# Expert weights in transfers of 64 partitions by 8 KB instead of 128 partitions by 4 KB

## The chip, the core and the metric

The kernel runs on one NeuronCore of a Trainium2 chip. The metric is the device time of one execution in microseconds (us). "The profile" is one profiled execution of the same program; its rows are counted in us from its first instruction. Engines: PE is TensorE (matmuls; PEld its weight loads), DVE is VectorE, ACT is ScalarE, POOL is GpSimd, SP is SyncE, which here does nothing but issue transfers. Transfers run on the core's 16 DMA engines.

## What is computed

Two blocks over 256 tokens of width 1024, float32 throughout. The first block has two layers, each a sequence mixer (a gated recurrence, then stick-breaking attention) with memory attention beside it, an output projection with a norm, and a mixture of experts with a norm. The second block is one layer of attention with forget gates, a convolutional feed-forward of width 2816 and a gated embedding. The change touches the weights of the mixture of experts alone:

```python
def hier_moe(x, w_group, b_group, w_router, b_router, w_gate, w_up, w_down):
    # top-1 of 4 groups, then top-2 of its 4 experts: gates (T, 16)
    ...
    h = jax.nn.silu(jnp.einsum('td,edf->tef', xf, w_gate)) * jnp.einsum('td,edf->tef', xf, w_up)
    y = jnp.einsum('tef,efd->td', h * gates[:, :, None].astype(h.dtype), w_down)
```

w_gate and w_up are 16 x 1024 x 256 and w_down is 16 x 256 x 1024, for each of the two layers: 3 MB an expert, 48 MB a layer, all of it fetched from device memory once.

## The kernel before, in words

**Engines and order.** Each engine runs one instruction stream written out by hand, in the order of the layers, and the streams meet at semaphores. SP's stream is the order of all weight transfers. `put` (from line 384) fetches the dense weights into a ring of four 1 MB buffers, `raw` (128 partitions by four slots of 2048 floats); ACT rounds each into `w_hi` (line 1639) and DVE takes the rest into `w_lo` (line 2116), and PE multiplies with both parts.

**The expert stage.** The expert weights are used unsplit, so `raw`, `w_hi` and `w_lo` together serve as twelve 1 MB *slabs* (`hi_as_raw` and `lo_as_raw` are the latter two seen as plain float32). `STREAM` (lines 72 to 77) lists the 48 slabs of a layer: for each of the 8 pairs of experts two halves of the gate and up weights of both experts ("G", four slabs), then the down weights of both experts of the pair before ("D", two slabs). SP's `experts` (line 392) walks through it. For slab n it waits until the buffer is free: for the first twelve until the dense weights there are used up (`lo_split`, `half_used`), and beyond until PE has used slab n - 12 and its neighbour (`slab_used`). Slabs 10 and 11 of layer 0 wait for `counted` besides. Then it issues two transfers of 512 KB that both count on the slab's semaphore, 16 each:

```python
if kind == "G":
    for i in range(2):
        cs = slice(HALF // 2 * i, HALF // 2 * i + HALF // 2)
        sp.dma_start(r[:, cs], gate_up[e, half, :, cs]).then_inc(landed, 16)
else:
    v = r.rearrange("p (k n) -> p k n", k=2)
    for i in range(2):
        sp.dma_start(v[:, i, :], wd[e, :, i, :]).then_inc(landed, 16)
```

Each covers all 128 partitions and half of every partition's row, so one run of bytes is 4 KB. `gate_up` has been laid out by the host as it lands (16 experts x 2 halves x 128 partitions x 2048); `w_down` is read as it is given, where partition p of slab half k is row 128 k + p.

**PE in the stage.** `short_path` runs `gate_up(p)` and then `down(p - 1)` for the eight pairs. Both wait (`weights_in`) until both slabs of a pair of experts have landed in full, 32 counts a slab. A slab takes 4 matmul steps for either expert, the two experts side by side in the two halves of the array; between them PE gathers the tokens of the next pair and scatters the results of the last (`hooks`). After `down(7)`, `close_sums` adds the last pairs up from `y_hi` and `y_lo`, which ACT (line 1639) and DVE (line 2137) make from PE's sums.

**After the stage.** SP goes on with `put`: in layer 0 with `w_kv_shared`, in layer 1 with `attn_w_in_2` (after the 256 KB of `p_2`). In ACT's stream the rounding of the first of these weights stands ahead of the last `y_hi`. The two rows of norm gains (`gain<-in_ln_ffn_g` and `_b`, 512 KB each) come on ACT's own queue while the first slabs are fetched.

Of the kernel before, what the change touches and what calls it, by code (L numbers as in the profile page):

```python
# [27 lines left out]
P = 128  # L28
# [24 lines left out]
HALF = 2048  # L53
# [55 lines left out]
def both(n):  # L109

    return n - n % 2 + 2
# [101 lines left out]
def build(nc, a, out, FAST_LIMIT=SLOTS):  # L213
    ctx = ExitStack()
    with ctx:
# [12 lines left out]
        def sem(name):  # L228
            if name not in sems:
                sems[name] = ctx.enter_context(nc.semaphore(name))  # L230
            return sems[name]
# [108 lines left out]
        def slab(layer, n):  # L340

            part, slot = kept_at(layer, n % SLABS)
            return {"raw": raw, "hi": hi_as_raw, "lo": lo_as_raw}[part][:, slot, :]

        def slab_sem(layer, n):

            part, slot = kept_at(layer, n % SLABS)
            return raw_in[slot] if part == "raw" else slab_in[n % SLABS - RING]
# [8 lines left out]
        def _(sp):  # L357
# [35 lines left out]
            def experts(layer):  # L393

                base = AT[f"E{layer}"]
                assert h == base
                gate_up = a["gate_up"][layer]
                wd = a["w_down"][layer].rearrange("e (k p) n -> e p k n", p=P)
                for n, (kind, e, half) in enumerate(STREAM):
                    s = n % SLABS  # L400
                    if layer == 0 and n == SLABS - 2:
                        sp.wait_ge(sem("counted"), 2)
                    if n >= SLABS:
                        sp.wait_ge(slab_used, len(STREAM) * layer + both(n - SLABS))
                    elif s < RING:
                        sp.wait_ge(lo_split, base - RING + s + 1)
                    else:
                        sp.wait_ge(half_used, base - RING + (s - RING) // 2 + 1)
                    r, landed = slab(layer, n), slab_sem(layer, n)
                    if kind == "G":  # L410
                        for i in range(2):
                            cs = slice(HALF // 2 * i, HALF // 2 * i + HALF // 2)
                            sp.dma_start(r[:, cs], gate_up[e, half, :, cs]).then_inc(landed, 16)
                    else:
                        v = r.rearrange("p (k n) -> p k n", k=2)
                        for i in range(2):
                            sp.dma_start(v[:, i, :], wd[e, :, i, :]).then_inc(landed, 16)

            def gains(g, b, n):

# [8 lines left out]
            for c in range(2):  # L429
                cs = slice(512 * c, 512 * c + 512)  # L430
# [17 lines left out]
            for layer in range(2):  # L448
                if layer:
                    for half in range(2):  # L450
                        put(tm(a["w_kv_shared"], SEQ_W, half))
                    put(fm(a["w_kv_shared"], SEQ_W + 512))
                    for j in range(3):
                        put(fm(a["w_kv_shared"], 256 * j))
                        put(fm(a["b_w_in"][0], 256 * j))
                        if j == 0:
                            put(fm(a["b_w_in"][0], SEQ_W))
                    for half in range(2):
                        for j in range(2):
                            put(tm_rows(a["w_o"][1], 512 * j, O_ROWS[1][half]))  # L460
                else:
                    for half in range(2):
                        for j in range(2):
                            put(tm(a["w_o"][0], 512 * j, half))
                    put(fm(a["w_mem_kv"][1], 0))
                    sp.wait_ge(sem("mixed_ready"), 4)
                gains(a["ln_mix_g"][layer], a["ln_mix_b"][layer], 2 * layer)
                experts(layer)
# [28 lines left out]
            for n, (b, at, width) in enumerate(GATE_TILES):  # L497
                sp.wait_ge(sem("result"), n + 1)
                cs = slice(at, at + width)
# [1610 lines left out]
        def _(dve):  # L2110
# [773 lines left out]


_FULL = ["x", "mem", "a_w_in", "a_gnorm", "b_w_in", "w_kv_shared", "w_mem_kv", "w_o", "ln_mix_g", "ln_mix_b",
         "ln_ffn_g", "ln_ffn_b", "w_down", "p_2", "attn_w_in_2", "attn_b_f_2", "attn_w_out_2",
         "ln_mix_g_2", "ln_mix_b_2", "ffn_w_up_2", "ffn_w_down_2", "ln_ffn_g_2", "ln_ffn_b_2", "ple_w_proj_2",
         "ple_w_gate_2", "ple_b_gate_2"]

# [36 lines left out]
```

## Time and profile before

| | |
|---|---|
| time, median of 3 runs | 907.32 us (905.35 to 909.91) |
| span of the profiled execution | 902.7 us; its time was not taken apart from it |
| PE busy | 881.5 us (98%) |
| PE weight loads | 678.2 us (75%) |
| DVE, ACT, POOL busy | 502.8, 391.4, 35.2 us |
| TensorE clock granted | 1.00 of full speed |
| read from device memory | 203.87 MB, 227 GB/s over the span |
| queue of SP | 202.14 MB, 62.6% of the time of 16 DMA engines |

The span runs from the first to the last instruction. What a run takes around it (start and end of the program) is not in the trace: the three runs lie 2.7 to 7.2 us above this span, the median 4.6 us. The page cuts the span into 40 slices of 22.6 us and gives for each the busy share of each engine in tenths, the granted TensorE clock and what the DMA engines moved. A PE that is busy has something in its pipeline; a chain of waits names what the end of the program hung on.

### The profile page before, as it was taken

Reading aid. Unit: us, or ns where it says so; the run is one execution under the profiler, and the core shown is the slowest. Engines: PE = TensorE matmul, PEld = TensorE weight load, DVE = VectorE, ACT = ScalarE, POOL = GpSimd, SP = SyncE. Lnnn points to the kernel's source line nnn. Section 1 sums busy time; section 2 is a strip of 40 time slices with the busy share of each in tenths; the row PEclk is TensorE's granted clock in tenths of the full one; section 3 lists DMA queues with packets and bytes.
Section 4 is the critical chain, followed back from the end, with each engine's and each line's share of the span. In section 5 each row is a group of like instructions: output and inputs, shape, how many; then the busy total and the mean of one; then the engine's idle time right before and its main releaser. Section 6 shows DMA issues by size and latency. Waiting matters only on the chain.

```text
span 902.7 us, 13442 instructions
## 1 busy us (share of the span) xinstructions
PE 881.5 (98%) x5387; PEld 678.2 (75%) x5387; DVE 502.8 (56%) x752; ACT 391.4 (43%) x531; POOL 35.2 (4%) x73
## 2 busy tenths in 40 slices
PE   7999999989999999999999999999999999999998
PEld 6988998944543698878545446899877888888887
DVE  4798876711111965626211118465658777777576
ACT  4755654232221536551322215435545666655441
POOL 7100010000000000000000000000001000000010
PEclk9999999999999999999999999999999999999999
DMA  9934417979999574329599996354543655546611
GB/s 319 318 96 139 141 47 263 341 254 411 409 409 401 179 242 169 100 89 351 190 411 409 409 403 216 122 181 166 176 152 118 219 192 192 187 139 233 234 47 46
DMA packets 102828, 205.78 MB, mean 228 GB/s; under 512 B 6896, under 2 KB 57840, under 8 KB 102768
## 3 DMA queue, kind: packets, MB, share of 16 engines
q1 hardware_dynamic: 101184, 202.14, 62.6%
q10 hardware_dynamic: 1584, 2.81, 1.0%
q8 instruction: 42, 0.69, 0.3%
q14 instruction: 18, 0.15, 0.0%
HBM read 203.87 MB, written 1.05 MB: 227 GB/s over the span
## 4 chain that ended last, share of the span: by engine, by line
PE 83%; DVE 5%; DMA 5%; ACT 4%; issue 2%; SPq 1%; DVEq 0%; ACTq 0%
PE psum L709 80%; DVE w_lo L2116 2%; DMA raw<-in_w_kv_shared 2%; ACT w_hi L1639 1%; DMA raw<-in_attn_w_in 1%; DMA raw<-in_a_w_in 1%; ACT arena L1639 1%; SPq L361 1%; PE psum L817 1%; DMA x_res<-in_x 1%; ACT x_slots L1639 0%; PE psum L1504 0%; PE psum L922 0%; DVE xt L2137 0%; PE psum L1018 0%
## 5 line engine op out<-in xcount | busy, mean ns | idle before, releaser
L709 PE MATMUL psum<-xt,w_hi 128*128 128x256 f32 (+1 forms) x1056 | 253.8, 321 | 3.9 <-DVEq L2831 1.7
L2116 DVE TENSOR_TENSOR w_lo<-raw,w_hi 128x2048 fp32r<-128x2048 f32 x88 | 200.7, 2287 | 47.4 <-ACT w_hi L1639 44.3
L709 PE MATMUL psum<-xt,w_lo 128*128 128x256 f32 x704 | 198.2, 282 | 0.0
L709 PEld LDWEIGHTS psum<-xt,w_hi 128*128 128x128 f32 x1056 | 177.1, 190 | 19.4 <-issue 2.7
L1639 ACT ACTIVATE w_hi<-raw 128x2048 fp32r<-128x2048 f32 (+1 forms) x90 | 170.1, 1892 | 38.8 <-PE psum L709 23.4
L709 PEld LDWEIGHTS psum<-xt,w_lo 128*128 128x128 f32 x704 | 134.1, 191 | 0.0
L709 PE MATMUL psum<-w_hi,xt 128*128 128x512 f32 (+1 forms) x368 | 112.8, 379 | 0.0
L1639 ACT ACTIVATE arena<-psum 128x512 f32<-128x512 f32 (+2 forms) x70 | 40.8, 601 | 124.9 <-PE psum L709 82.6
L709 PE MATMUL psum<-hi_as_raw,x_slots 128*64 128x512 f32 x176 | 80.8, 596 | 0.0
L709 PE MATMUL psum<-lo_as_raw,x_slots 128*64 128x512 f32 x176 | 80.8, 596 | 0.0
L709 PEld LDWEIGHTS psum<-w_hi,xt 128*128 128x128 f32 x368 | 67.3, 189 | 12.6 <-DVE xt L2137 1.1
L2601 DVE SCALAR_TENSOR_TENSOR arena<-psum,slot_gate,arena 128x256 f32<-128x256 f32 x16 | 7.7, 484 | 114.8 <-ACT arena L1639 114.8
L709 PE MATMUL psum<-w_hi,mt_hi 128*128 128x512 f32 (+1 forms) x184 | 69.8, 380 | 0.3 <-DVE mt_lo L2137 0.3
L709 PE MATMUL psum<-w_lo,xt 128*128 128x512 f32 (+1 forms) x184 | 68.4, 372 | 0.0
L709 PE MATMUL psum<-w_lo,mt_hi 128*128 128x512 f32 (+1 forms) x184 | 68.3, 371 | 0.0
L709 PE MATMUL psum<-w_hi,mt_lo 128*128 128x512 f32 (+1 forms) x184 | 68.3, 371 | 0.0
L1639 ACT ACTIVATE arena<-arena 128x512 f32<-128x512 f32 (+3 forms) x62 | 40.3, 656 | 57.2 <-DVE arena L2245 22.7
L709 PEld LDWEIGHTS psum<-hi_as_raw,x_slots 128*64 128x64 f32 x176 | 23.0, 137 | 44.4 <-issue 43.3
L582 POOL TENSOR_TENSOR rstd<-var_eps,neg_half 128x1 f32<-128x1 f32 (+1 forms) x15 | 16.5, 1104 | 838.6 <-DVE var_eps L2389 586.5
L709 PE MATMUL psum<-arena 128*128 128x128 f32 (+2 forms) x316 | 40.5, 302 | 2.9 <-DVE arena L2265 1.0
L2137 DVE TENSOR_TENSOR y_lo<-psum,y_hi 128x512 fp32r<-128x512 f32 x32 | 21.7, 689 | 36.5 <-ACT y_hi L1639 36.5
L709 PEld LDWEIGHTS psum<-arena 128*128 128x128 f32 (+1 forms) x316 | 34.3, 189 | 8.9 <-issue 3.4
(267 smaller groups left out, 1245.0 us busy)
## 6 DMA issues: line engine op xcount, KB each, us to landing
hi_as_raw<-in_gate_up SPq DMA_DIRECT2D x44, 512.0 KB, 7.7
lo_as_raw<-in_gate_up SPq DMA_DIRECT2D x44, 512.0 KB, 9.1
raw<-in_ffn_w_up SPq DMA_DIRECT2D x44, 512.0 KB, 4.5
raw<-in_gate_up SPq DMA_DIRECT2D x40, 512.0 KB, 6.8
raw<-in_a_w_in SPq DMA_DIRECT2D x26, 512.0 KB, 7.5
raw<-in_w_down SPq DMA_DIRECT2D x24, 512.0 KB, 10.5
raw<-in_attn_w_in SPq DMA_DIRECT2D x24, 512.0 KB, 5.0
raw<-in_ffn_w_down SPq DMA_DIRECT2D x22, 512.0 KB, 4.1
```

The costliest lines, as they stand in the source:

```text
L361: sp.dma_start(dst, src).then_inc(raw_in[slot], 16)
L582: pool.tensor_tensor(rstd[:, cols], var_eps[:, cols], neg_half[:, cols], ALU.pow)\
L709: return pe.matmul(o, l, r, start=start, stop=stop, skip_group_check=skip)
L817: last = pe.transpose(turned(b)[:, k // 4, k % 4, :], x_res[:, b, P * k:P * k + P], ident[:])
L1639: return act.activation(o, i, f, **kw)
L2116: return dve.tensor_tensor(w_half(h, w_lo), w_half(h, raw), w_half(h, w_hi).bitcast(F32), ALU.subtract).then_inc(lo_split, 1)
L2137: return dve.tensor_tensor(o, whole, hi.bitcast(F32), ALU.subtract)
L2601: dve.scalar_tensor_tensor(ex_h[:, p % 2, 0, :], psum[:, gu_bank(p), 256:512], slot_gate[:, p // 2 % 2, p % 2:p % 2 + 1], ex_s[:, p % 2, 0 ...
```

## The change

The columns are no longer halved, the partitions are: each slab now comes as one transfer into partitions 0 to 63 and one into partitions 64 to 127, each with the whole row of 2048 floats (8 KB) of every partition. For this the host lays out the down weights like the others, as `down` (2 x 16 x 128 x 2048). Number, size and order of the transfers, their semaphores and all waits stay.

```diff
@@ -395,7 +395,7 @@
                 base = AT[f"E{layer}"]
                 assert h == base
                 gate_up = a["gate_up"][layer]
-                wd = a["w_down"][layer].rearrange("e (k p) n -> e p k n", p=P)
+                down = a["down"][layer]
                 for n, (kind, e, half) in enumerate(STREAM):
...
                     r, landed = slab(layer, n), slab_sem(layer, n)
-                    if kind == "G":
-                        for i in range(2):
-                            cs = slice(HALF // 2 * i, HALF // 2 * i + HALF // 2)
-                            sp.dma_start(r[:, cs], gate_up[e, half, :, cs]).then_inc(landed, 16)
-                    else:
-                        v = r.rearrange("p (k n) -> p k n", k=2)
-                        for i in range(2):
-                            sp.dma_start(v[:, i, :], wd[e, :, i, :]).then_inc(landed, 16)
+                    src = gate_up[e, half] if kind == "G" else down[e]
+                    for i in range(2):
+                        ps = slice(P // 2 * i, P // 2 * i + P // 2)
+                        sp.dma_start(r[ps, :], src[ps, :]).then_inc(landed, 16)
@@ -2905,6 +2901,8 @@
+    down = np.asarray(inputs["w_down"]).reshape(2, 16, 2, 128, 1024).transpose(0, 1, 3, 2, 4)
+    arrays["down"] = np.ascontiguousarray(down).reshape(2, 16, 128, 2048)
```

SP's stream at the head of layer 0's expert stage, before: a row is a number of like transfers in a row, with the partitions and floats of one (`gain` is the norm gains just ahead of the stage, the two rows left out repeat those above them, `in_w_down` and `in_gate_up` are the weights in device memory).

```order
L424 DMA gain<-in_ln_mix_b 128x1024
L413 DMA raw<-in_gate_up 128x1024 x8
L413 DMA hi_as_raw<-in_gate_up 128x1024 x2
L413 DMA lo_as_raw<-in_gate_up 128x1024 x2
...
L417 DMA hi_as_raw<-in_w_down 128x1024 x2
L417 DMA lo_as_raw<-in_w_down 128x1024 x2
```

The same place in the changed kernel:

```order
L420 DMA gain<-in_ln_mix_b 128x1024
L413 DMA raw<-in_gate_up 64x2048 x8
L413 DMA hi_as_raw<-in_gate_up 64x2048 x2
L413 DMA lo_as_raw<-in_gate_up 64x2048 x2
...
L413 DMA hi_as_raw<-in_down 64x2048 x2
L413 DMA lo_as_raw<-in_down 64x2048 x2
```

Every transfer of the stage stands in its old place with its new shape; nothing moves past anything, and the streams of the other four engines read alike before and after.

## Rows read from the trace of the kernel before

**Rows 1.** The page: busy time, and the span in 40 slices.
```profile
PE 881.5 (98%) x5387; PEld 678.2 (75%) x5387; DVE 502.8 (56%) x752; ACT 391.4 (43%) x531; POOL 35.2 (4%) x73
...
GB/s 319 318 96 139 141 47 263 341 254 411 409 409 401 179 242 169 100 89 351 190 411 409 409 403 216 122 181 166 176 152 118 219 192 192 187 139 233 234 47 46
```

**Rows 2.** Stretches: us, then busy us of each engine, clock, DMA share, GB/s.
```profile
20.00:30.00 10.00, 10.00 (x86) 10.00 (x86) 5.65 (x6) 4.79 (x4) 4.59 (x8) 1.00 1.08 360
180.00:190.00 10.00, 6.90 (x59) 5.00 (x59) 2.15 (x9) 5.95 (x10) 0.00 (x0) 1.00 0.37 125
200.00:289.00 89.00, 89.00 (x485) 41.72 (x482) 14.55 (x28) 17.37 (x34) 0.00 (x0) 1.00 1.03 409
455.00:540.00 85.00, 85.00 (x466) 40.46 (x464) 14.55 (x28) 16.54 (x32) 0.00 (x0) 1.00 1.03 408
```

**Rows 3.** The chain of waits, layer 0's expert stage: start us, us, what.
```profile
227.71 15.07 PE psum L709 x89
242.78 0.22 PE psum L1196 x2
243.00 14.64 PE psum L709 x74
257.64 0.22 PE psum L1196 x2
...
277.71 0.38 SPq L361
278.09 0.04 issue
278.13 13.92 DMA raw<-in_w_kv_shared
292.05 0.02 issue
292.07 1.07 ACT w_hi L1639
```

**Rows 4.** Waits of SP's queue from 195 to 290: total, times, longest.
```profile
SPq L413 <- PE psum L709: 35.8, 10, 6.7
SPq L417 <- PE psum L709: 12.2, 6, 3.9
```

**Rows 5.** The last four w_down transfers of layer 0 (274 to 277).
```profile
L417 SPq DMA_DIRECT2D lo_as_raw<-in_w_down x2: 430/896/1362, 275.1 to 275.5; - x2
...
DMA to landing us min/median/max: 9.7/11.8/13.8
```

**Rows 6.** The last eight w_down transfers of layer 1 (519 to 530).
```profile
L417 SPq DMA_DIRECT2D lo_as_raw<-in_w_down x4: 430/432/432, 520.0 to 527.0; - x4
...
DMA to landing us min/median/max: 8.9/11.2/13.4
```

**Rows 7.** Timeline of PE: down(7) begins, and what follows it (both layers).
```profile
289.46 0.59 PE L709 MATMUL psum<-hi_as_raw,ht 128*64 128x512 f32 x1
...
294.52 0.50 PE L709 MATMUL psum<-y_hi,ht_lo 128*128 128x512 f32 x1 [1.08 <-ACT y_hi L1639]
295.24 0.50 PE L709 MATMUL psum<-y_lo,ht_lo 128*128 128x512 f32 x1 [0.22 <-DVE y_lo L2137]
...
540.95 0.59 PE L709 MATMUL psum<-hi_as_raw,ht 128*64 128x512 f32 x1
...
545.71 0.50 PE L709 MATMUL psum<-y_lo,ht_lo 128*128 128x512 f32 x1 [0.23 <-DVE y_lo L2137]
```

**Rows 8.** Timeline of ACT at the end of layer 0's stage.
```profile
292.07 1.91 ACT L1639 ACTIVATE w_hi<-raw 128x2048 fp32r<-128x2048 f32 x1 [2.01 <-DMA raw<-in_w_kv_shared]
293.89 1.07 ACT L1639 ACTIVATE y_hi<-psum 128x512 fp32r<-128x512 f32 x2
```

**Rows 9.** Timeline of SP, the starts of both streams: start us, us for all.
```profile
144.44 9.21 SPq L413 DMA_DIRECT2D raw<-in_gate_up  x8
...
185.39 0.80 SPq L413 DMA_DIRECT2D hi_as_raw<-in_gate_up  x2
...
190.91 2.45 SPq L413 DMA_DIRECT2D raw<-in_gate_up  x4
...
406.54 0.80 SPq L413 DMA_DIRECT2D hi_as_raw<-in_gate_up  x2
...
442.40 1.95 SPq L413 DMA_DIRECT2D raw<-in_gate_up  x4
```

**Rows 10.** The raw, hi and lo gate_up transfers from 144 to 168.
```profile
DMA to landing us min/median/max: 4.1/6.5/9.4
```

More of the change, by code:

```diff
@@ L2886 @@
 _FULL = ["x", "mem", "a_w_in", "a_gnorm", "b_w_in", "w_kv_shared", "w_mem_kv", "w_o", "ln_mix_g", "ln_mix_b",
-         "ln_ffn_g", "ln_ffn_b", "w_down", "p_2", "attn_w_in_2", "attn_b_f_2", "attn_w_out_2",
+         "ln_ffn_g", "ln_ffn_b", "p_2", "attn_w_in_2", "attn_b_f_2", "attn_w_out_2",
          "ln_mix_g_2", "ln_mix_b_2", "ffn_w_up_2", "ffn_w_down_2", "ln_ffn_g_2", "ln_ffn_b_2", "ple_w_proj_2",
```

## The prediction

> **What bounds the kernel now.** First the page: PE is busy in 98% of the span, and the bandwidth line has two plateaus of 401 to 411 GB/s, four slices each, which are the expert stages of the two layers [rows 1]. Everywhere else it lies lower. Then the stretches: in both plateaus PE is busy for the whole stretch while the DMA engines are busy for the whole stretch too, a share of 1.03 at 409 and 408 GB/s [rows 2]. So two engines are full at once, and the question is which has slack. PE takes 14.64 + 0.22 us for one pair of experts and 15.07 + 0.22 for another, about 15.1 on average [rows 3]. A pair is six slabs, twelve transfers of 524,288 bytes; at 409 GB/s one takes 1.28 us and twelve take 15.4. The supply is thus slower than the demand, and only the ring of twelve slabs, filled before the stage begins, carries the stage to its end. SP still waits for PE to free slabs, 35.8 + 12.2 us between 195 and 290 [rows 4], but no longer for want of work for the DMA engines: their queue stays full. How much of the lead is left at the end: the last down weights of layer 0 are issued at 275.5 and land 13.8 us later, at 289.3 [rows 5], and down(7), which needs them, begins at 289.46 [rows 7]. In layer 1: 527.0 at the latest and 13.4, so 540.4 [rows 6], against 540.95 [rows 7]. **The transfers have 0.1 and 0.5 us of slack.** Whatever makes a transfer longer is paid in full, and whatever makes it shorter can only give back the waits behind it. Those are small: the next weights land at 292.05 at the end of the chain's transfer of 13.92 us [rows 3], ACT rounds them first for 1.91 us and makes y_hi after that [rows 8], and PE waits 1.08 + 0.22 us for y_hi and y_lo in layer 0 and 0.23 in layer 1 [rows 7].
>
> **What changes.** 96 transfers a layer keep their bytes, order and waits. Two properties change: a run of bytes is 8 KB and not 4, and a transfer touches 64 partitions and not 128. Everything else is priced at nothing: the host's layout of the down weights is done before the launch, the other engines' streams are the same, and issuing is SP's work, 0.80 us for two [rows 9], beside transfers that take longer.
>
> *The longer run.* A stretch of 1 KB runs (a_w_in, behind a full queue) moves 360 GB/s and one of 4 KB runs 409 [rows 2]. Sixteen engines side by side: 1024 x 16 / 360 = 45.5 ns a run and 4096 x 16 / 409 = 160.2 ns. The line through both is 7.3 ns a run and 0.0373 ns a byte, which gives 313 ns for 8 KB, 418 GB/s, 1.253 us a transfer: 2% less. Slabs 10 to 47 of a layer follow each other without a gap (they start at 185.39 in layer 0 [rows 9]), 76 transfers, so the end would come 76 x 0.027 = 2.1 us earlier. Of it PE sees only its waits behind the stage, 1.3 + 0.2 = 1.5 us.
>
> *Half the partitions.* No row of this trace has a transfer of 64 partitions. What the rows say is that nearly all rates tend to one ceiling, which the line above puts at 16 / 0.0373 = 429 GB/s for endless runs. A ceiling per byte sits either in the DMA engines themselves, and then it doesn't matter where they write, or on the way into the partitions, and then a transfer that writes to half of them has half of it. The bounds: 1.25 us a transfer (only the run counts) and twice today's 1.28, 2.56 us. The trace can't choose. The Trainium skill (SBUF — State Buffer, "Door 1: The DMA port swizzle") holds that the second is so: partitions 0 to 63 lie behind 8 of 16 ports, and it gives 196 GB/s for them against 328 for all 128. By that figure a transfer would take 2.67 us, and the sum below would be 223 us and the time 1130. Its section "Can I just issue two DMAs to hit both halves?" adds that two such transfers side by side gained 6%, as they serialize. No run here shows either yet.
>
> I take the ceiling to be on the way in, since the change alternates between the halves and nothing in the kernel makes engines take different halves at once. But not quite at half speed: SP hands out a transfer in 0.4 us (0.80 for two [rows 9]), so engines that share a way can be up to half of that, 0.2 us, out of step, and for that long the one ahead is already in the other half alone. Twice 1.253 less 0.2 is **2.3 us a transfer**, 228 GB/s.
>
> *The sum.* A transfer that finds the queue empty lands 4.1 us after its issue [rows 10], 2.8 us more than its 1.28. Layer 0: the first is issued at 144.44 [rows 9]; 96 of them and the two rows of gains from ACT's queue (2 x 1.28 = 2.6) bring the last to 144.4 + 2.8 + 96 x 2.3 + 2.6 = 370.6. There is no gap: slab 10, which may not go before 185.39, finds 20 transfers ahead of it that last until 195.8, and slab 12 is free to go at 190.91 [rows 9]. Against 289.3: **+81.3 us**. Layer 1: slabs 0 to 3 come early as now; from 406.54, 88 transfers: 406.5 + 2.8 + 88 x 2.3 + 2.6 = 614.3, and slab 12, free at 442.40 [rows 9], finds the queue full until 448.7. Against 540.4: **+73.9 us**. PE's work after the last slab follows as now, and so do the waits there. Together +155.2; the span of 902.7 becomes 1057.9, and the median, which stood 4.6 us above it, about 1062. PE would wait for weights in most of its steps, some 55% busy (15.1 of 12 x 2.3 = 27.6 us a pair). The granted clock stays 1.00 in a stretch with PE busy 6.90 of 10 us [rows 2]; if it fell to 1.2 GHz at 55%, a pair would be 30.2 us of PE and a stage 8 x 2.6 = 21 us longer, which the upper end holds.
>
> **The rivals.**
>
> *Serialized halves, the forecast, 0.54.* For it: the rates tend to one ceiling per byte, and the two halves of a slab are issued one behind the other into one queue. Against it: no row shows the ceiling to lie on the partitions' side. Its own range: 0.1 us a transfer is 18.4 us of the sum (96 + 88), so from 2.05 us (1016) to 2.56 (1110).
>
> *The halves overlap, 0.12.* The queue is up to ten transfers deep (13.8 us to landing [rows 5]), so the 16 engines may drift apart by a whole transfer and more; were they spread evenly, each would share its way half of the time: 1.5 x 1.253 = 1.88 us. Layer 0 ends at 144.4 + 2.8 + 180.5 + 2.6 = 330.3, +41.0; layer 1 at 577.3, +36.9; 985 us. Against it: a transfer needs all engines, so the pair that is most in step sets the pace.
>
> *Only the run length counts, 0.29.* The ceiling is in the DMA engines, and where they write is all one. Then the transfers last 1.253 us and the two waits behind the stages, 1.5 us, go: 906 us, no change that can be seen. This is the case on the other side, and its place is the pair of slabs before down(7): it holds as long as a transfer takes no more than 1.28 us. For it speaks that 1.03 of share is full use of the engines themselves.
>
> *Faster, 0.05.* Longer runs relieve more than the line says, and the weights behind the stages arrive so early that ACT and DVE, which share the chain elsewhere, get ahead. PE is idle 902.7 - 881.5 = 21 us in all [rows 1], and only 1.5 of it hangs on these transfers, so over 4.5 us is unlikely.
>
> **How the numbers follow.** A measurement of this kernel tells about 0.5%, 4.5 us, from no change. Slower by more: 0.54 + 0.12 = 0.66. Within: 0.29. Faster: 0.05. The time is that of the likeliest case, 1062. The range must hold 8 in 10; without the case of no change it would leave out 0.34, so it reaches from 904 to 1110, and the likeliest case's own range is 1016 to 1110.
>
> **What would show it.** Right: two plateaus at 210 to 260 GB/s, seven to eight slices each, the DMA share still near 1; PE with waits on DMA for the slabs all through the stage; issue to landing of 20 us and more; the last down weights at 345 to 390 us. Then the rest of the program shifted and otherwise alike. Wrong: plateaus of 409 or more of the old length. With 418 GB/s the rival of the run length has it, and the waits of 1.08 and 0.23 us should be gone; with 260 to 400 the halves overlap, and PE's waits begin late in the stage. A lower granted clock inside the stage would point to the upper end.

## The result, and the profile after

The changed kernel takes 1068.88 us (median of 6 runs, 1057.58 to 1079.85), the kernel before 905.22 us (median of 6 runs beside them, 904.19 to 909.91). The ratio is 1.1744, with a 95% interval of 1.171 to 1.1779: **slower by 17%**. The ratio is that of the fast runs and leaves out the two of the six that took 1077.47 and 1079.85 us. The profiled execution took 1057.58 us, the least of the six, with a span of 1055.8, so 1.8 us lie around the span. All numbers below that come from a profile are compared with its own span, 902.7 before and 1055.8 after: 153.1 us more.

The page of the changed kernel, the lines that answer to [rows 1], with the granted clock and the DMA share of each slice:

```profile
PE 933.2 (88%) x5387; PEld 693.7 (66%) x5387; DVE 503.3 (48%) x752; ACT 391.4 (37%) x531; POOL 37.4 (4%) x73
...
PEclk9999999898998699999898888789999999999999
DMA  9733269999999935549999999973644276464821
GB/s 322 263 120 120 81 185 224 235 242 265 283 275 278 282 125 170 147 91 223 214 223 223 223 225 227 226 249 122 196 148 153 85 236 198 160 201 157 275 83 40
```

The two plateaus of 401 to 411 GB/s, four slices each, have become nine slices of 185 to 283 and nine of 214 to 249, while the DMA line reads 9 in eight slices of either (the first slice of one and the last of the other lie partly outside the stage): the engines are as busy as they were and move between a half and 70% as much. PE is busy in 88% of the span and not in 98%. The digits of PEclk, all full before in the stretches of [rows 2], now dip to 6 and 7 inside the stages.

Stretches of the changed kernel; the columns are those of [rows 2], us first, then the busy time of PE, PEld, DVE, ACT and POOL, the granted clock, the DMA share and GB/s:

```profile
150.00:180.00 30.00, 30.00 (x197) 27.20 (x196) 19.61 (x38) 5.47 (x9) 2.15 (x2) 1.00 1.01 222
185.00:205.00 20.00, 15.82 (x74) 7.34 (x76) 0.98 (x3) 1.96 (x4) 0.00 (x0) 0.74 1.02 237
210.00:350.00 140.00, 109.18 (x498) 47.70 (x496) 15.03 (x29) 17.08 (x34) 0.00 (x0) 0.88 1.02 267
225.00:245.00 20.00, 16.98 (x74) 7.66 (x70) 2.89 (x5) 2.56 (x5) 0.00 (x0) 0.83 1.02 249
265.00:285.00 20.00, 16.09 (x90) 8.05 (x89) 2.36 (x5) 3.15 (x6) 0.00 (x0) 0.92 1.02 284
...
560.00:640.00 80.00, 50.32 (x231) 22.42 (x228) 7.01 (x14) 7.89 (x15) 0.00 (x0) 0.85 1.02 224
```

A transfer has 524,288 bytes, so the rates read as durations: 222 GB/s are 2.36 us, 284 are 1.85, 224 are 2.34. Before, it was 1.28. Layer 1 keeps the low rate to its end; layer 0 begins with it and gains later, to 249 GB/s from 225 us and 284 from 265. The full share with half the rate says that the DMA engines don't idle: they are held up.

What PE waited for (total us, times, longest), in the changed kernel:

```profile
PE psum L705 <- DMA lo_as_raw<-in_gate_up: 38.4, 13, 5.3
PE psum L705 <- DMA lo_as_raw<-in_down: 22.9, 6, 5.8
PE psum L705 <- issue: 16.1, 6, 6.7
PE psum L705 <- ACT y_hi L1635: 15.6, 2, 8.4
```

The chain of waits in layer 0's stage, which answers to [rows 3]:

```profile
226.92 32.56 DMA lo_as_raw<-in_gate_up
...
259.74 8.02 PE psum L705 x37
...
272.72 33.18 DMA lo_as_raw<-in_gate_up
...
320.77 35.24 DMA raw<-in_w_kv_shared
```

Before, the chain in this stage was PE's and held one transfer, the 13.92 us of w_kv_shared at its end. Now three transfers of 33 to 35 us cover 101 of the 129 us from 227 to 356. A long transfer in a chain is not a slow one: it stands behind what lies in the queue, fourteen transfers or more at 1.9 to 2.4 us each.

The end of both stages. The last down weights, issued at 317.1 and 646.9, took 36.4 and about 41.9 us to land, so 353.5 and 688.8. Before it was 289.3 [rows 5], and 539.0 in layer 1: the last one issued there, at 527.0, took 12.0 us, and the 13.4 of [rows 6] belong to another. Behind them stand the first dense weights. SP's last issues of layer 0 and how long they took to land, then the timelines of ACT and PE in the changed kernel:

```profile
L413 SPq DMA_DIRECT2D lo_as_raw<-in_down x2: 1425/2212/3000, 315.6 to 317.1; - x2
...
DMA to landing us min/median/max: 31.5/34.0/36.4
```

```profile
356.04 1.91 ACT L1635 ACTIVATE w_hi<-raw 128x2048 fp32r<-128x2048 f32 x1 [15.13 <-DMA raw<-in_w_kv_shared]
357.85 1.06 ACT L1635 ACTIVATE y_hi<-psum 128x512 fp32r<-128x512 f32 x2
358.80 0.39 ACT L1635 ACTIVATE ht<-psum 128x256 f32<-128x256 f32 x1
```

```profile
358.48 0.79 PE L705 MATMUL psum<-y_hi,ht_lo 128*128 128x512 f32 x1 [7.29 <-ACT y_hi L1635]
...
369.73 2.02 PE L705 MATMUL psum<-zeros_r 128*128 128x512 f32 x8
...
694.47 0.80 PE L705 MATMUL psum<-y_hi,ht_lo 128*128 128x512 f32 x1 [8.36 <-ACT y_hi L1635]
...
704.98 2.02 PE L705 MATMUL psum<-zeros_r 128*128 128x512 f32 x8
```

The eight products with zeros_r are the first work of PE behind a stage, a good mark for its end: 369.73 and 704.98. Before:

```profile
303.68 2.01 PE L709 MATMUL psum<-zeros_r 128*128 128x512 f32 x8
...
554.15 2.01 PE L709 MATMUL psum<-zeros_r 128*128 128x512 f32 x8
```

So layer 0 costs 66.1 us, layer 1 another 84.8, and 2.3 of the 153.1 come behind it.

### The profile page after: what moved, and what is told of

It is laid out like the page before. It is cut to its first block, busy times and chain, and to the rows that moved or that the text cites. A ratio compares the mean times of both kernels' runs of the same rounds, so it can differ in the third digit from the quotient of the medians.

```text
span 1055.8 us, 13442 instructions
## 1 busy us (share of the span) xinstructions
PE 933.2 (88%) x5387; PEld 693.7 (66%) x5387; DVE 503.3 (48%) x752; ACT 391.4 (37%) x531; POOL 37.4 (4%) x73
## 4 chain that ended last, share of the span: by engine, by line
PE 67%; DMA 21%; DVE 4%; issue 3%; ACT 3%; SPq 2%; ACTq 0%; DVEq 0%
PE psum L705 65%; DMA lo_as_raw<-in_gate_up 13%; DMA raw<-in_w_kv_shared 3%; DMA raw<-in_attn_w_in 3%; DVE w_lo L2112 2%; SPq L413 1%; ACT w_hi L1635 1%; ACT arena L1635 1%; SPq L361 1%; PE psum L813 1%; DMA x_res<-in_x 1%; PE psum L803 0%; ACT x_slots L1635 0%; PE psum L1500 0%; PE psum L918 0%
## 5 line engine op out<-in xcount | busy, mean ns | idle before, releaser
L705 PE MATMUL psum<-hi_as_raw,x_slots 128*64 128x512 f32 x176 | 98.4, 702 | 38.4 <-DMA lo_as_raw<-in_gate_up 38.4
L705 PE MATMUL psum<-lo_as_raw,x_slots 128*64 128x512 f32 x176 | 98.7, 704 | 0.0
L705 PEld LDWEIGHTS psum<-hi_as_raw,x_slots 128*64 128x64 f32 x176 | 25.3, 157 | 93.5 <-issue 92.4
L705 PE MATMUL psum<-hi_as_raw,ht 128*64 128x512 f32 x80 | 47.6, 751 | 22.9 <-DMA lo_as_raw<-in_down 22.9
L705 PE MATMUL psum<-raw,x_slots 128*64 128x512 f32 x160 | 42.5, 668 | 14.5 <-issue 14.5
## 6 DMA issues: line engine op xcount, KB each, us to landing
raw<-in_gate_up SPq DMA_DIRECT2D x40, 512.0 KB, 11.7
```

Of the source, the lines that this page charges most:

```text
L705: return pe.matmul(o, l, r, start=start, stop=stop, skip_group_check=skip)
```

## The experiments

Every kernel below is the changed kernel with the edit shown. "The rate" is that of the stretches of the stages. Where one run is given, its time stands beside 905 to 909 us for the kernel before on the same chip. The experiments ran on three chips, so times of different experiments are compared by their ratios to the kernel before.

### Which property costs: four kernels

**The whole slab in one transfer** (128 partitions, one run of 8 KB each; the `nop`, an instruction without work, adds the 16 counts that the second transfer brought):

```diff
-                    for i in range(2):
-                        ps = slice(P // 2 * i, P // 2 * i + P // 2)
-                        sp.dma_start(r[ps, :], src[ps, :]).then_inc(landed, 16)
+                    sp.nop().then_inc(landed, 16)
+                    sp.dma_start(r, src).then_inc(landed, 16)
```

> One transfer of 128 partitions by 8 KB (1 MB) for each slab: the long run without the half partitions. Theory P (what costs is that a transfer reaches only half of the partitions): a slab takes 2 x 1.25 us or less, both expert stages run at 410 to 425 GB/s, the waits of PE behind the stages (1.1 and 0.2 us) shrink, and the time is 902 to 905 us. Rival L (what costs is the 8 KB run, or that there are half as many runs for each engine to have under way): as slow as the change, 1050 to 1080 us at 220 to 280 GB/s.

**64 partitions, two runs of 4 KB each** (the host puts the two halves of the columns apart):

```diff
-                        sp.dma_start(r[ps, :], src[ps, :]).then_inc(landed, 16)
+                        sp.dma_start(r[ps, :].rearrange("p (c n) -> p c n", c=2),
+                                     src[:, ps, :].rearrange("c p n -> p c n")).then_inc(landed, 16)
```

> 64 partitions by two runs of 4 KB for each transfer, so half the partitions with the run length of the kernel before (the host lays out gate, up and down weights in column halves for it). Theory P: as slow as the change, 1050 to 1085 us, 220 to 280 GB/s in the stages. Rival L: 903 to 908 us at 409 GB/s.

**128 partitions, two runs of 2 KB each**, so the same bytes in the same number of transfers, with runs shorter than before (here too the host lays the pieces apart):

```diff
-                        ps = slice(P // 2 * i, P // 2 * i + P // 2)
-                        sp.dma_start(r[ps, :], src[ps, :]).then_inc(landed, 16)
+                        cs = slice(HALF // 2 * i, HALF // 2 * i + HALF // 2)
+                        sp.dma_start(r[:, cs].rearrange("p (c n) -> p c n", c=2),
+                                     src[2 * i:2 * i + 2].rearrange("c p n -> p c n")).then_inc(landed, 16)
```

> 128 partitions by two runs of 2 KB for each transfer, same transfers and waits otherwise. It measures what a slightly longer transfer costs. By the line through 1 KB and 4 KB runs a 2 KB run takes 83.8 ns, a transfer 1.34 us instead of 1.28 (391 GB/s). Theory Z (the stage has no slack, a longer transfer is paid in full): the first dense weights behind each stage land 76 x 0.06 = 4.6 us later, PE's wait there grows by as much, 913 to 916 us. Rival S (the last down weights have 7 us of slack, since down(7) begins at 296.3 and not at 289.5, and the stage as a whole can take some of it): 905 to 908 us.

**64 partitions, every second one**: the even ones in the first transfer, the odd ones in the second, one run of 8 KB each, as in the change:

```diff
-                        ps = slice(P // 2 * i, P // 2 * i + P // 2)
-                        sp.dma_start(r[ps, :], src[ps, :]).then_inc(landed, 16)
+                        sp.dma_start(r[i::2, :], src[i::2, :]).then_inc(landed, 16)
```

> The halves are the even and the odd partitions instead of 0 to 63 and 64 to 127: 64 partitions by 8 KB as in the change, but spread over all. Theory P in its plain form (64 partitions are half of 128, whichever): 1050 to 1085 us. Theory W (blocks of partitions have a way in of their own, and only a transfer that stays in one half reaches half of the ways): about 903 to 925 us, near 400 GB/s, if every engine then has a way for itself; if the engines still meet in pairs on the way in while they are in step, anything between, up to the time of the change.

It was run again against the kernel before in five rounds:

> The even and the odd partitions as halves, timed. Theory W: the stages run at 417 to 420 GB/s and PE's waits for y_hi behind them are gone (1.3 us in layer 0, 0.2 in layer 1), which is 1.5 us; other waits that hang on the DMA queue may give some more. 901 to 904 us, a ratio of 0.995 to 0.999 to the kernel before, and the same within 1 us as whole slabs in one transfer (903.7).

What they gave:

| kernel | partitions x run | us | GB/s, layer 0 / layer 1 |
|---|---|---|---|
| before | 128 x 4 KB | 905.22 | 409 / 408 |
| changed | 64 (a block) x 8 KB | 1068.88 | 222 to 284 / 224 |
| 64 x two 4 KB | 64 (a block) x 4 KB | 1058.59 (one run) | 222 to 277 / 222 |
| whole slab | 128 x 8 KB | 903.65, ratio 0.9972 (0.9952 to 0.9993) | 420 / 414 |
| 128 x two 2 KB | 128 x 2 KB | 916.22, ratio 1.0123 (1.0079 to 1.0167) | 386 / 387 |
| even and odd | 64 (every second) x 8 KB | 903.02, ratio 0.9973 (0.9953 to 0.9992) | 420 / 417 |

Stretches of the kernel with 64 partitions and 4 KB runs:

```profile
150.00:180.00 30.00, 30.00 (x197) 27.23 (x196) 19.47 (x38) 5.48 (x9) 2.16 (x2) 1.00 1.03 222
...
560.00:640.00 80.00, 53.75 (x229) 22.71 (x226) 6.52 (x12) 7.89 (x15) 0.00 (x0) 0.81 1.03 222
```

The same in the kernel of even and odd partitions (the five rounds):

```profile
205.00:225.00 20.00, 20.00 (x117) 9.69 (x112) 4.12 (x9) 3.99 (x8) 0.00 (x0) 1.00 1.01 419
...
455.00:540.00 85.00, 85.00 (x466) 40.45 (x464) 14.55 (x28) 17.12 (x33) 0.00 (x0) 1.00 1.02 417
```

Read against each other, two rows a time. Between the first kernel of this section and the change only the cut into blocks differs, and with it the number of transfers: 903.65 and 1068.88. With the cut left and the run back at 4 KB nothing is regained: 222 GB/s at the start of layer 0 and 222 in layer 1, where the change has 222 and 224. And 64 partitions as a number are innocent, and so is the number of transfers: 64 that are spread over all 128 run at 417 to 420 GB/s, with the same count, size and run length as in the change. **What costs is that the partitions of one transfer are all from one half of the memory**, 0 to 63 or 64 to 127. No run took a block that lies across the middle, such as 32 to 95, so the runs don't show that the border lies at 64. The Trainium skill (SBUF — State Buffer, "Door 1: The DMA port swizzle") puts the two halves behind 8 of 16 ports each; the trace agrees in kind, with 222 to 224 GB/s for its 196. By its table of ports the even partitions alone reach all 16, and the 417 to 420 of even and odd bear that out.

The run length alone, 128 partitions throughout: 387 GB/s with 2 KB, 409 with 4 KB, 414 to 420 with 8 KB. In the kernel with 2 KB PE waits again at the end of layer 0's stage, in its timeline:

```profile
296.43 0.56 PE L706 MATMUL psum<-y_hi,ht_lo 128*128 128x512 f32 x1 [4.53 <-ACT y_hi L1636]
```

and this wait with its like in layer 1, 10.2 us for y_hi together where the kernel before has 1.1, is most of the 11 us that it loses. The other way, the 8 KB runs of the whole slab leave this wait at nothing, which with the waits of [rows 7] is about 1.3 us; the ratio of 0.9972 is 2.5 us.

### Why layer 0 gains on the way

From 225 us on, layer 0 moves 249 to 284 GB/s though nothing about its transfers changes. (Between 185 and 205 us the 237 GB/s are in part the two transfers of norm gains.) The thought: the 16 DMA engines start a transfer together while the queue is nearly empty, and then all want the same half. As some fall behind, they are in the other half while the rest are in the first, and both halves take data. To test it, SP lets the queue run empty three times a layer, which puts the engines back in step:

```diff
+                    if n in (12, 24, 36):
+                        sp.wait_ge(slab_sem(layer, n - 1), landed_at(layer, n - 1))
                     r, landed = slab(layer, n), slab_sem(layer, n)
```

> The change, and before slabs 12, 24 and 36 of each layer SP waits until the slab issued last has landed, so that the queue runs empty and all engines start the next transfer together. In the change layer 0 ran at 235 and then 280 GB/s, layer 1 at 223. Theory T (two engines share a way; in step they halve each other, out of step they overlap, and layer 0 was out of step by chance): layer 0 falls back to 222 to 230 GB/s, its last down weights land 20 to 30 us later, layer 1 changes by the three empty queues alone (about 3 us each), 1085 to 1105 us. Rival A (layer 0's weights lie better in device memory, or something else that belongs to the layer): layer 0 keeps about 275 GB/s, only the empty queues are added, 1070 to 1085 us.

It took 1098.61 us. Its stretches in layer 0:

```profile
225.00:245.00 20.00, 14.48 (x62) 5.58 (x61) 2.32 (x5) 2.77 (x5) 0.00 (x0) 0.83 1.01 223
...
265.00:285.00 20.00, 15.60 (x76) 7.78 (x76) 1.18 (x3) 1.82 (x4) 0.00 (x0) 0.83 0.88 191
285.00:305.00 20.00, 12.68 (x40) 5.08 (x41) 2.29 (x4) 1.58 (x3) 0.00 (x0) 0.74 1.01 221
305.00:325.00 20.00, 12.24 (x55) 5.10 (x53) 1.87 (x3) 3.16 (x6) 0.00 (x0) 0.83 1.01 220
```

The share of 0.88 is where the queue ran empty; on both sides of it the rate is 220 to 223 and never more. The last down weights of layer 0 land at 387.7, 34.2 us later than in the changed kernel's profile; the three empty queues themselves are some 9 us of this, by the missing share (0.85, 0.88 and 0.87 for 1.02 in stretches of 20 us). So emptying the queue takes the gain away. That fits the thought; that the engines are in different halves during the gain is inferred from it, as no view of the profile shows which partition an engine writes.

Time with a full queue is not enough for the gain, though. The changed kernel, ACT's issues of the norm gains in both layers, and a stretch of layer 1:

```profile
175.07 0.33 ACTq L1813 DMA_DIRECT2D gain<-in_ln_ffn_g  x1
...
494.07 0.34 ACTq L1813 DMA_DIRECT2D gain<-in_ln_ffn_g  x1
```

```profile
520.00:680.00 160.00, 112.87 (x520) 50.24 (x518) 16.55 (x32) 18.41 (x37) 0.00 (x0) 0.88 1.01 224
```

For 160 us behind the empty queue of layer 1 the queue is full and the rate stays at 224. What differs is the order of two events. In layer 0 the gains, which come from the other queue and go to all 128 partitions, land by 195.4 in a queue that stays full, and the rate from 205 us on is 235 and more (229 and more in the four profiles). In layer 1 they land by 515.0, and the queue runs empty behind them (slab 12 is issued at 516.30). The other profiles with blocks have the same order. It may be these two transfers that set the engines apart, and the next empty queue that puts them back; no run moved them, so this stays open.

Next, three kernels meant to shift some engines on purpose, by a copy from device memory to device memory in so few rows that only some engines should take part in it (no view shows which did): eight rows of 32 KB in front of slabs 0 and 10 (4 and 12 in layer 1), then eight and four rows behind the layer's first expert slab.

```diff
+                    if n in ((0, 10), (4, 12))[layer]:
+                        row = a["gate_up"][layer][e, half].rearrange("(a b) n -> a (b n)", a=8)[:, 0:4 * HALF]
+                        sp.dma_start(a["spare"][2 * layer + (n >= 10)], row).then_inc(sem("shifted"), 16)
```

> The change, and ahead of slabs 0 and 10 of layer 0 and 4 and 12 of layer 1 SP issues one transfer of 8 rows by 32 KB from device memory to device memory. If it runs on 8 of the 16 engines, as many bytes on each as one expert transfer, these 8 are then one transfer behind the other 8. Theory T with pairs made of one engine of each eight: the two halves of a slab are then fetched side by side, 380 to 418 GB/s in at least the first part of a stage, and the time falls to 905 to 990 us, depending on how long the shift lasts. Rival N (the pairs lie within the eights, or the order of the engines doesn't matter, and only the number of partitions under way does): the rate stays at 223 to 280 GB/s, and the time is that of the change plus four short transfers, 1055 to 1095 us.

It took 1065.5 us, with 221 GB/s from 150 to 180, 259 from 210 to 350 and 223 in layer 1: as without the copy.

```diff
-                    if n in ((0, 10), (4, 12))[layer]:
+                    if n == (1, 5)[layer]:
```

> As before it, but the extra transfer of 8 rows by 32 KB stands behind the first expert transfer of layer 0 (and behind that of slab 4 in layer 1), where the queue is not empty: in the run before it began on idle engines 0.8 us ahead of the next transfer, and the eight engines it ran on were only about 0.5 us late. Now they should be at least 1.2 us late. Theory T with the pairs across the two eights: 380 to 418 GB/s from there until the queue next runs empty, the first slabs land every 2.6 us instead of 4.7, time below 1040 us. Rival N (pairs within the eights): 220 to 225 GB/s at 166 to 176 us as in the change, 1055 to 1095 us.

> The same with 4 rows by 32 KB, which should put four engines one transfer behind. Theory T with pairs that lie within the first eight (each of the four late engines paired with one of the other four): the four pairs of the first eight run at full rate, the other eight at half; a transfer needs all of them, so the slabs land no earlier, but the DMA engines move more bytes in some stretches while the late ones catch up. Theory T with pairs across the eights: the same, four pairs of eight. In either case 1050 to 1090 us and 220 to 290 GB/s. Only if landing gets faster than in the change is the picture of fixed pairs wrong.

With eight rows there (1069.36 us):

```profile
150.00:180.00 30.00, 30.00 (x197) 27.20 (x196) 19.63 (x38) 5.47 (x9) 2.16 (x2) 1.00 1.02 232
```

With four rows (1076.04 us) it was 220 from 150 to 180 and 236 from 210 to 350. There is no jump towards the full rate in the early stretch, 232 and 220 for 222. With eight rows theory T thus fails and the time is that of rival N; four rows came out as all the pairings foretold (1050 to 1090 us, 220 to 290 GB/s) and decide nothing. These copies do not bring the rate up; whether they shifted the engines at all, and how engines and partitions go together in a transfer of 64 partitions, stays open.

**The changed kernel once more**, for the spread:

> The changed kernel once more, unchanged, for its profile. Its first profile moved 267 GB/s from 210 to 350 us in layer 0 (224 from 560 to 640 in layer 1); a kernel with the same transfers, but another order on ACT behind them, moved 235. Theory (whether the engines fall out of step is chance, and that is the spread of 1057.6 to 1079.9 us): layer 0 shows some rate between 222 and 270 GB/s, and the time follows it: 100 MB at 235 instead of 267 GB/s is some 18 us from 210 on (140 us of it), so about 1057 at 267 and 1070 to 1080 at 225 to 235. Rival (the order on ACT slowed the transfers): 265 to 270 GB/s again, and the time within 3 us of 1058.

It took 1070.35 us. Its stretches:

```profile
210.00:350.00 140.00, 103.08 (x478) 45.62 (x476) 14.55 (x28) 17.32 (x34) 0.00 (x0) 0.89 1.02 245
...
560.00:640.00 80.00, 54.10 (x240) 25.05 (x238) 6.79 (x13) 8.87 (x17) 0.00 (x0) 0.85 1.01 222
```

The same kernel moved 267 GB/s once and 245 the other time from 210 to 350; the last down weights of layer 0 landed 11.5 us later (365.0 for 353.5), and the span is 12.8 us longer. Two kernels with the same transfers, below, moved 235 both. So the gain of layer 0 is there each time and its size changes from execution to execution, without a known cause; between these two profiles it makes 11.5 of 12.8 us, and it may well be the spread of the changed kernel's times, 22 us where the kernel before has 6. It also takes the word from the late rates of the three shifted kernels (259, 239, 236), which lie within this spread. The 220 to 223 of the emptied queue lie below all of it, and so do its last down weights, which come 16 us behind the latest of the four profiles (371.5) and 34 behind the earliest, some 9 us of either being the empty queues. The Trainium skill (SBUF — State Buffer, "Can I just issue two DMAs to hit both halves?") holds that two transfers to the two halves gain 6% side by side. Here, in a deep queue of such transfers, layer 1 gained nothing to speak of (222 to 224 GB/s), and layer 0 moved 235 to 267 for 222 from 210 to 350 us, 6 to 20%, with 28% in its best stretch (284).

### The price of the wait before y_hi

PE stands 7.29 and 8.36 us before y_hi, because ACT rounds the first dense weights ahead of it. What is this order worth? First y_hi alone goes ahead:

```diff
                         if p:
+                            round_y(p - 1)
                             if p == PAIRS - 1:
                                 round_to(base + 1)
-                            round_y(p - 1)
```

> The changed kernel, with one order turned round on ACT at the end of each expert stage: it makes y_hi of pair 6 first and rounds the first dense weights behind the stage after it. In the changed kernel PE stood 7.29 us (at 358.48) and 8.36 us (at 694.47) before that y_hi, since ACT waited 15.13 and 15.91 us for the dense weights first. Theory (the wait is the order on ACT and not the data): both waits go. PE then waits for the last down weights instead, landed at 353.5, so down(7) begins at about 354 and not 360.8, some 6 us a layer earlier, and the span is about 12 us shorter, 1044, if the transfers come as before. Rival 1 (something behind it is late anyway, the dense weights themselves, landed at 356.0 and 692.0): PE's wait moves behind down(7), in front of the first products with the dense weights or of the pieces that ACT rounds late, and the span is within 3 us of 1056. Rival 2 (the time of the changed kernel moves by over 10 us from run to run): the trace's waits decide and not the time. The last down weights land where they did, 351 to 356 and 686 to 692, by all of them.

1068.81 us (median of 4, 1063.11 to 1074.21), a ratio of 1.1762 (1.1692 to 1.1831). PE's timeline:

```profile
376.15 1.12 PE L705 MATMUL psum<-hi_as_raw,ht 128*64 128x512 f32 x1 [5.66 <-ACT ht L1635]
...
385.98 2.02 PE L705 MATMUL psum<-zeros_r 128*128 128x512 f32 x8
```

The last line of the timeline is the mark of the stage's end. The wait for y_hi is gone and one of 5.66 us (7.19 in layer 1) for ht, the h of pair 7, has come, made by ACT behind the same rounding. A miss, by an instruction that the expectation had not counted. So both go ahead:

```diff
                         if p:
-                            if p == PAIRS - 1:
-                                round_to(base + 1)
                             round_y(p - 1)
                     take_h(PAIRS - 1)
                     round_to(base + 2)
```

> The changed kernel, where ACT rounds none of the dense weights behind the stage until it has made y_hi of pair 6 and taken h of pair 7 (ht); they come right behind that. With y_hi alone moved ahead, PE's waits of 7.29 and 8.36 us before y_hi became waits of 5.66 and 7.19 us for ht, made behind the same rounding. Theory (all of it is what stands behind the rounding on ACT): with both ahead, PE waits in front of down(7) for no more than 1 us, or for the last down weights, and the end of the stage follows the last down weights by 13 to 15 us where the changed kernel took 20 (353.5 to 371.6, with 18.1, and 688.8 to 706.8): about 5 us a layer. Rival (the dense weights are what is late): PE waits 5 us or more further on, before y_hi of pair 7 or before the first product with the dense weights, and nothing is gained. The time itself, 1045 to 1070, moves by more than this from run to run.

1061.79 us (median of 5, 1057.84 to 1075.65), a ratio of 1.1664 (1.1634 to 1.1694). PE's timeline:

```profile
371.26 0.61 PE L705 MATMUL psum<-hi_as_raw,ht 128*64 128x512 f32 x1 [0.59 <-DMA lo_as_raw<-in_down]
378.79 0.79 PE L705 MATMUL psum<-y_hi,ht_lo 128*128 128x512 f32 x1 [2.75 <-ACT y_hi L1635]
381.34 0.80 PE L705 MATMUL psum<-y_lo,ht_lo 128*128 128x512 f32 x1 [1.75 <-DVE y_lo L2131]
...
385.71 2.01 PE L705 MATMUL psum<-zeros_r 128*128 128x512 f32 x8
```

Now down(7) begins right behind its weights (landed at 371.1), and 4.5 us come back before y_hi and y_lo of pair 7, since the dense weights land at 373.6 and ACT rounds two pieces of them there. From the last down weights to zeros_r it is:

| kernel | layer 0 | layer 1 |
|---|---|---|
| before | 303.68 - 289.3 = 14.4 | 554.15 - 539.0 = 15.1 |
| changed | 369.73 - 353.5 = 16.2 | 704.98 - 688.8 = 16.2 |
| changed, once more | 380.57 - 365.0 = 15.6 | 717.69 - 700.5 = 17.2 |
| y_hi ahead | 385.98 - 371.5 = 14.5 | 721.53 - 707.2 = 14.3 |
| y_hi and ht ahead | 385.71 - 371.1 = 14.6 | 722.86 - 707.1 = 15.8 |

With the rounding first the mean of the four is 16.3 us, with y_hi first 14.8. (The last expectation counts to a later product, 371.6 and 706.8, and so has 18.1 where this table has 16.2.) The waits of 7.29 and 8.36 us are thus worth about 1.5 us a layer and not the 5 or 6 expected. In layer 0 of the last kernel down(7) begins 0.2 us behind its weights, and 7.3 in the changed kernel, but of that 4.5 us are lost again before y_hi and y_lo of pair 7, and 2.5 in the 16 products behind down(7): without these waits they take 6.4 us, 3.8 in the changed kernel, most of them 0.63 us each for 0.40, at the lower clock (granted 0.50 from 379 to 385 us). Down(7) itself gives back 1.5 (3.6 us for 5.1), which leaves 1.6. The medians (1068.88, 1068.81, 1061.79) don't settle it: two of them agree, and the third is 7 us lower. By the ratios, 1.1744 (from 1.171) and 1.1664 (to 1.1694), the last kernel is a little faster than the change. Its profile is of an execution of 1075.65 us, the longest of its five, so where the 7 us are stays open.

### The best version

Even and odd partitions at 903.02 us and the whole slab at 903.65 us are both 0.27 to 0.28% faster than the kernel before, with intervals that just leave 1 out; a gain that small is hardly more than the noise. They can't be told from each other. Whoever wants the 8 KB runs has them with either.

## Why the prediction was right, and where not

**The mechanism held.** "I take the ceiling to be on the way in" is what the four kernels show for blocks of 0 to 63 and 64 to 127, and the rival of the run length fell with them. That "a transfer that writes to half of them has half of it" is too wide: half of them taken as every second partition has all of it. Forecast 1062, measured 1068.88; slower, as given the larger chance.

**That the number came so close is partly luck.** In the profile layer 0 cost 17 us less than its term and layer 1 11.7 more, and the two misses, taken apart below, mostly cancel. And the "4.6 us above" the span was not a time around the span: every execution lies 1.7 to 1.8 us above its own span, and the rest was the difference between the profiled execution and the median one.

**The longer run.** The line through two stretches gave 418 GB/s for 8 KB on all partitions, measured 414 to 420; for 2 KB it gives 7.3 + 76.4 = 83.7 ns, 391 GB/s, measured 387.

**2.3 us a transfer** was measured at 2.34 in layer 1 and 1.85 to 2.36 in layer 0. The number is right, its reason less so: 0.2 us was taken off twice 1.253 for engines out of step. In step, with the queue just emptied, it is 2.36; out of step, it goes down to 1.85, the 1.88 of the rival of overlapping halves. The 0.4 us an issue from which the 0.2 us came is itself 0.55 with 64 partitions. So layer 1 fits the forecast's case and the best stretches of layer 0 the rival's; that both are one mechanism, which differs in how far the engines have drifted apart, is inferred.

**Layer 0, +81.3.** The last down weights came 353.5 - 289.3 = 64.2 us later. The term was too large by 17, since the rate rose on the way. On the other runs of the same transfers (landed at 365.0, 371.5, 371.1) it would be 75.7 to 82.2, close to the sum.

**Layer 1, +73.9.** The last down weights were 149.8 later, 85.6 more than layer 0's 64.2, so the term was too small by 11.7. 1.4 of it is the base, 539.0 and not 540.4, and 1.9 lie between the layers (slab 4 is issued at 472.60 for 406.54, 66.1 us later and not 64.2). The other 8.4 are in the stage: 216.2 us from slab 4's issue to the last landing, where the sum had 207.8. Of them 88 transfers at 2.34 and not 2.3 make 3.5. Then the queue ran empty, which the step "finds the queue full" had excluded: slab 12 went at 516.30, and the sixteen transfers ahead of it were through at 472.6 + 2.8 + 16 x 2.36 = 513.2. SP and the stretch, in the changed kernel:

```profile
516.30 3.37 SPq L413 DMA_DIRECT2D raw<-in_gate_up  x4
```

```profile
510.00:520.00 10.00, 10.00 (x65) 5.98 (x63) 0.49 (x2) 1.46 (x3) 0.00 (x0) 0.97 0.88 191
```

A share of 0.88 for 1.02 is 1.4 us of idle engines. The last 3.5 us have no row of their own.

**Slack.** This step failed in its reading and did no harm to the sum. "Down(7), which needs them, begins at 289.46" took the wrong pair: those products use the down weights of pair 6, issued at 267.7 to 269.2 and landed up to 15.0 us later, by 284.2, and down(7) begins later. The last two of the four issues, how long the four took to land, and down(7) in PE's timeline, in the kernel before:

```profile
L417 SPq DMA_DIRECT2D lo_as_raw<-in_w_down x2: 661/869/1077, 268.5 to 269.2; - x2
...
DMA to landing us min/median/max: 11.1/13.2/15.0
```

```profile
296.27 0.64 PE L709 MATMUL psum<-hi_as_raw,ht 128*64 128x512 f32 x1
```

The last down weights thus had 7.0 us of slack. What has none is the transfer right behind them, w_kv_shared at 292.05 [rows 3], for which ACT and so y_hi stand, and since it lands 2.5 to 2.8 us behind the last down weights in both kernels (356.04 after), every microsecond was paid all the same: the last down weights come 64.2 us later in layer 0 and the stage ends 66.1 later. The kernel with 2 KB runs shows it: its down weights land at 291.2, 5 us before down(7) would need them, and PE stands 4.53 us for y_hi.

**The clock.** That it "stays 1.00", read from a stretch with PE busy 6.90 of 10 us, did not carry over (the upper end of the range allowed for it): from 185 to 205 it was 0.74 and in layer 1's stage 0.85, at the lower of its levels, 1.2 GHz, for stretches behind PE's waits, where a product takes 1.06 us for 0.59. PE's busy time of 933.2 us for 881.5 is this for the most part (products with x_slots from hi_as_raw and lo_as_raw alone take 98.4 and 98.7 us for 80.8 each). That it hardly lengthened the stage is read from the DMA share, 1.01 to 1.02 in every stretch but those where the queue ran empty: the supply went on while PE was slow. No run tested it alone.

**Half busy.** "Some 55%" was 63% in layer 1 (50.32 of 80) and 78% in layer 0 (109.18 of 140), of it much at the lower clock.

**Issue to landing** of 20 us and more: 27 to 37 us in the second half of layer 0, a median of 41 and at most 43.5 in layer 1's. **The rest of the program** is shifted and else alike: 2.3 us of the 153.1 are behind layer 1's stage.

## What to carry to other kernels

When a tile is cut into several transfers, cut it across the bytes of a partition, or by every second partition, and not into partitions 0 to 63 and 64 to 127: the blocks ran at 222 GB/s, at best 284, and the other cuts at 387 to 420, with the same bytes, the same count and the same queue. Longer runs are worth little once they have 4 KB (409 to 414 or 420), and only if PE waits for them somewhere. And before pricing slack, look up which transfer the waiting instruction needs: by the issue times on the queue, and what stands behind it on every engine that takes part, for the wait may be for the transfer after.

## What the runs showed that was not expected

The rate of the blocks drifts between 222 and 284 GB/s within one execution, differently each time, and fell back to 220 to 223 in the run in which the queue was emptied; the kernel's time spreads over 22 us.

At the start of a stage PE waits for something that the profile doesn't name ("issue"), and longer when the DMA engines are held up. The changed kernel, layer 0 and 1, then the kernel before:

```profile
187.84 5.39 PE L705 MATMUL psum<-raw,x_slots 128*64 128x512 f32 x12 [6.52 <-issue]
...
506.99 4.60 PE L705 MATMUL psum<-raw,x_slots 128*64 128x512 f32 x12 [6.71 <-issue]
```

```profile
184.31 2.80 PE L709 MATMUL psum<-raw,x_slots 128*64 128x512 f32 x12 [3.10 <-issue]
```

In layer 1 the kernel before has no such wait. Even and odd partitions have one of 1.8 us at the longest. It may be the loading of instructions (the profile counts 60 instruction packets among the DMA's, on two queues of their own), but no run here tests that. PE begins the stages 3.4 and 6.7 us later for it. Most of that is hidden, as the transfers go on meanwhile; what shows is the 1.4 us of empty queue in layer 1, and in the other profiles with blocks the queue runs empty there too.

SP takes 1.11 us for two issues of 64 partitions and not 0.80, blocks or every second one alike. The changed kernel:

```profile
162.39 1.11 SPq L413 DMA_DIRECT2D hi_as_raw<-in_gate_up  x2
```

With much in flight an issue takes longer still. The three of w_kv_shared in the changed kernel, behind which SP has nothing urgent:

```profile
320.19 15.08 SPq L361 DMA_DIRECT2D raw<-in_w_kv_shared  x3
```
